# Expert keys beside the scatter: both parts of x in one 512-column matmul, the two column blocks added one step later

## What is computed

```python
def peer_ffn(n, w_q, sub_keys, expert_u, expert_v):
    """PEER: 8 product-key retrieval heads over N = 128^2 single-neuron experts."""
    ...
    experts = (i1 * PEER_KEYS + i2).reshape(T, PEER_HEADS * PEER_TOPK)
    gates = jax.nn.softmax(best, axis=-1).reshape(T, PEER_HEADS * PEER_TOPK).astype(n.dtype)
    ...
        u = expert_u[eb].astype(xb.dtype)
        act = jax.nn.gelu(jnp.einsum('td,tkd->tk', xb, u), approximate=False) * gb
        return jnp.einsum('tk,tkd->td', act, expert_v[eb].astype(xb.dtype))
```

## Time and profile before

| | us |
|---|---|
| median of 3 runs | 1690.45 |
| lowest, highest | 1690.38, 1691.01 |
| the profiled execution | 1690.79 |
| its span in the profile | 1689.0 |
| PE busy | 1658.7 |
| DVE busy | 1284.7 |
| ACT busy | 1028.3 |

### The profile page before, as it was taken

One profiled execution on the slowest core, in us unless ns is written; L12 is line 12 of the kernel. 1 busy time (PEld: TensorE's weight loads), 2 busy tenths in 40 slices (PEclk: granted clock), 3 DMA queues, 4 the chain that ended last, 5 costly groups with the idle time before them and its releaser, 6 DMA issues.

```text
span 1689.0 us, 34320 instructions
## 1 busy us (share of the span) xinstructions
PE 1658.7 (98%) x10835; PEld 1499.1 (89%) x10835; DVE 1284.7 (76%) x2365; ACT 1028.3 (61%) x1626; POOL 116.5 (7%) x105
## 2 busy tenths in 40 slices
PE   8999999999999999999999999999999999999998
PEld 7998889999999999988888888899788888878886
DVE  7867763899877777777777777799777777977776
ACT  7757555667556666655545455765576667766665
POOL 0025200444000000000000000100000000000000
PEclk9999999999999999999999999999999999999999
DMA  6543464777755555477787777542455554346553
GB/s 211 174 150 101 144 218 146 229 220 227 241 195 171 173 177 176 154 248 243 240 274 241 245 238 241 178 148 88 150 171 191 189 191 148 101 158 193 191 192 113
DMA packets 113294, 315.64 MB, mean 187 GB/s; under 512 B 12640, under 2 KB 44640, under 8 KB 112848
## 3 DMA queue, kind: packets, MB, share of 16 engines
q1 hardware_dynamic: 112032, 310.43, 56.5%
q0 software_dynamic: 880, 4.06, 0.7%
q10 hardware_dynamic: 320, 0.34, 0.1%
HBM read 296.43 MB, written 18.35 MB: 186 GB/s over the span
## 4 chain that ended last, share of the span: by engine, by line
PE 94%; DVE 2%; ACT 2%; DMA 1%; issue 1%; POOL 0%; SPq 0%; ACTq 0%; DVEq 0%; POOLq 0%
PE bank L273 12%; PE bank L274 12%; PE bank L275 12%; PE bank L338 11%; PE bank L339 10%; PE bank L340 10%; PE bank L294 10%; PE bank L298 5%; PE bank L1546 3%; PE bank L2003 2%; PE bank L330 1%; PE bank L332 1%; PE bank L331 1%; DVE wlo L245 1%; DMA h<-act_spill 0%
## 5 line engine op out<-in xcount | busy, mean ns | idle before, releaser
L245 DVE TENSOR_TENSOR wlo<-raw,whi 128x1024 fp32r<-128x1024 f32 x499 | 612.8, 1231 | 133.1 <-ACT whi L237 124.8
L237 ACT ACTIVATE whi<-raw 128x1024 fp32r<-128x1024 f32 x524 | 550.4, 1053 | 19.7 <-PE bank L332 14.0
L273 PE MATMUL bank<-x,whi 128*128 128x256 f32 (+3 forms) x1728 | 504.4, 292 | 2.5 <-DVE x L486 0.7
L275 PE MATMUL bank<-x,wlo 128*128 128x256 f32 (+3 forms) x1728 | 489.4, 283 | 0.0
L274 PE MATMUL bank<-x,whi 128*128 128x256 f32 (+3 forms) x1728 | 489.3, 283 | 0.0
L273 PEld LDWEIGHTS bank<-x,whi 128*128 128x128 f32 x1728 | 330.1, 191 | 6.1 <-issue 3.1
L274 PEld LDWEIGHTS bank<-x,whi 128*128 128x128 f32 x1728 | 330.7, 191 | 0.3
L275 PEld LDWEIGHTS bank<-x,wlo 128*128 128x128 f32 x1728 | 329.9, 191 | 0.0
L338 PE MATMUL bank<-whi,yhi 128*128 128x512 f32 x816 | 319.3, 391 | 1.0 <-DVE ylo L2343 0.7
L339 PE MATMUL bank<-wlo,yhi 128*128 128x512 f32 x816 | 318.1, 390 | 0.0
L340 PE MATMUL bank<-whi,ylo 128*128 128x512 f32 x816 | 317.6, 389 | 0.0
(11 more groups left out here) (324 smaller groups left out, 1712.5 us busy)
## 6 DMA issues: line engine op xcount, KB each, us to landing
raw<-in_stream SPq DMA_DIRECT2D x524, 512.0 KB, 3.4
act_spill<-h SPq DMA_DIRECT2D x124, 128.0 KB, 3.3
h<-act_spill SPq DMA_DIRECT2D x124, 128.0 KB, 3.2
h<-in_x SPq DMA_DIRECT2D x2, 512.0 KB, 5.1
arena<-in_keys POOLq DMA_DIRECT2D x1, 1024.0 KB, 6.3
h_spill<-h SPq DMA_DIRECT2D x1, 1024.0 KB, 7.9
arena<-h_spill POOLq DMA_DIRECT2D x1, 1024.0 KB, 7.3
arena<-in_g_final POOLq DMA_DIRECT2D x1, 512.0 KB, 9.3
```

Of the source, the lines that this page charges most:

```text
L237: nc.scalar.activation(whi[:, q * 1024:(q + 1) * 1024], raw[:, q * 1024:(q + 1) * 1024], ACT.Copy).then_inc(hi_ready, 1)
L245: nc.vector.tensor_tensor(wlo[:, q * 1024:(q + 1) * 1024], raw[:, q * 1024:(q + 1) * 1024], whi[:, q * 1024:(q + 1) * 1024].bitcast(F32), ...
L273: nc.tensor.matmul(bank[b][:, 0:T], whi[:, w], xhi[:, x], start=k == 0, stop=False)
L275: last = nc.tensor.matmul(bank[b][:, 0:T], wlo[:, w], xhi[:, x], start=False, stop=k == KT - 1)
```

## The change

Slabs 63 to 126 go through `up_halves` and no longer through `up`. The first pair of one-hot matmuls then stands between the 512-column and the 256-column matmuls, and the second behind the latter. The reading of a bank, one ACT instruction before, becomes three: ACT copies the right half to `HR` (`half_out`), DVE adds the left half to it and frees the bank (`half_sum`, in the step after), and ACT applies GELU in place (`half_gelu`, one step later than before). SP writes the activation to memory when the GELU is done (`u_act`), and the first product with the gates waits for it too. What that does to the order on the engines:

ACT in the steps of the scatter, before: one reading of the bank between two splits. `whi` is a high split, `arena` the store of G.

The diff, without the loops of the last steps on DVE and SP that only follow from it:

```diff
@@ in up_halves
             else:
                 for k in range(KT):
                     long(k)
+                if between:
+                    between()
                 pe.wait_ge(lo_ready, n + 1)
                 for k in range(KT):
                     last = short(k, k == KT - 1)
@@ in pe_peer
             def step(i, r):
-                up(pe, N_U + E1, U_U + E1, i, r, 4, SEQ, between=lambda: pair(i, r, 0))
+                up_halves(pe, N_U + E1, U_U + E1, i, r, 4, between=lambda: pair(i, r, 0))
                 pair(i, r, 1)
@@ in act_peer
+            def half_out(k0, i, r):
+                q = (k0 + r) % 4
+                act.wait_ge(slabs_done, at(N_U + k0, i, r, 4) + 1 + RING)
+                act.wait_ge(spill_sem(q), rounds(k0, i, r, 4) * 16 + 16)
+                nc.scalar.activation(HR[:, q * SEQ:(q + 1) * SEQ], bank[(U_U + k0 + r) % 2][:, SEQ:2 * SEQ], ACT.Copy)\
+                    .then_inc(s("u_half"), 1)
+
+            def half_gelu(k0, i, r):
+                q = slice((k0 + r) % 4 * SEQ, ((k0 + r) % 4 + 1) * SEQ)
+                act.wait_ge(up_evac, at(U_U + k0, i, r, 4) + 1 + 2)
+                nc.scalar.activation(HR[:, q], HR[:, q], ACT.Gelu).then_inc(s("u_act"), 1)
+
             split_hi(act, N_U + E1 + AHEAD, 0, 0, 4)
-            gelu(N_U + E1, U_U + E1, 0, 0)
+            half_out(E1, 0, 0)
 
             def step2(i, r):
                 split_hi(act, N_U + E1 + 1 + AHEAD, i, r, 4)
                 g_out(i, r)
-                gelu(N_U + E1 + 1, U_U + E1 + 1, i, r)
+                half_out(E1 + 1, i, r)
+                half_gelu(E1, i, r)
 
             steps(act, SCAT - 1, 4, step2)
             g_out(0, SCAT - 1)
+            half_gelu(E1 + SCAT - 1, 0, 0)
@@ in dve_peer
+            def half_sum(k0, i, r):
+                q = slice((k0 + r) % 4 * SEQ, ((k0 + r) % 4 + 1) * SEQ)
+                dve.wait_ge(s("u_half"), at(k0 - E1, i, r, 4) + 1)
+                nc.vector.tensor_tensor(HR[:, q], HR[:, q], bank[(U_U + k0 + r) % 2][:, 0:SEQ], ALU.add)\
+                    .then_inc(up_evac, 1)
+
+            def step(k0, i, r):
+                one_token(k0, i, r, 0)
+                one_token(k0, i, r, 1)
+                split_lo(dve, N_U + E1 + k0 + AHEAD, i, r, 4)
+                if k0:
+                    half_sum(E1 + k0 - 1, i, r)
+                one_token(k0, i, r, 2)
+                one_token(k0, i, r, 3)
+                four_tokens(k0 + 1, i, r)
@@ in prod
-                    dve.wait_ge(up_evac, U_U + KEYS - KEPT + k + 1 + 2)
+                    dve.wait_ge(s("u_act"), SCAT - KEPT + 1 + k + 1) if k < KEPT - 1 else \
+                        dve.wait_ge(up_evac, U_U + KEYS + 2)
@@ in sp_peer_loads
+            def store(k0, i, r):
+                load(sp, N_U + lead + k0, i, r, 4)
+                if k0 < E1:
+                    sp.wait_ge(up_evac, at(U_U + k0, i, r, 4) + 1 + 2)
+                else:
+                    sp.wait_ge(s("u_act"), at(k0 - E1, i, r, 4) + 1)
+                q = (k0 + r) % 4
+                sp.dma_start(act_dram(i, r, k0), HR[:, q * SEQ:(q + 1) * SEQ]).then_inc(spill_sem(q), 16)
```

More of the change, by code:

```diff
@@ L281, in up, with up_halves @@
             last.then_inc(slabs_done, 1)
-        def up_halves(pe, n0, u0, i, r, U, uU=None, x_ready=None):
+        def up_halves(pe, n0, u0, i, r, U, uU=None, x_ready=None, between=None):
             n, u = at(n0, i, r, U), at(u0, i, r, U if uU is None else uU)
@@ L1774, in dve_peer, with one_token @@
                     columns()
-            def one_token(i, r, y):
-                n = i * (4 * TPS) + r * TPS + y
+            def one_token(k0, i, r, y):
+                n = i * (4 * TPS) + (k0 + r) * TPS + y
                 dve.wait_ge(s("hot_free"), n - 2 + 1 + TPS)
@@ L1788, in four_tokens @@
                                         ALU.is_equal).then_inc(s("hot_b"), 1)
[L1790 to L1796, removed]
+            def half_sum(k0, i, r):
[12 more added lines that the diff above has]
+                four_tokens(k0 + 1, i, r)
             four_tokens(0, 0, 0)
-            steps(dve, SCAT - 1, 4, step)
+            step(0, 0, 0)
+            steps(dve, SCAT - 2, 4, lambda i, r: step(1, i, r))
             last = SCAT - 1
             for y in range(TPS):
-                one_token(last // 4, last % 4, y)
+                one_token(last, 0, 0, y)
                 if y == 1:
                     split_lo(dve, N_U + KEYS - 2 + AHEAD, 0, 0, 4)
+                    half_sum(E1 + last - 1, 0, 0)
+            half_sum(E1 + last, 0, 0)
             def prod(k0, i, r):
@@ L1881, in act_dram @@
                     t["act_spill"][bass.ds(k, 1)].rearrange("a p c -> (a p) c")
[L1883 to L1893, removed]
+            def store(k0, i, r):
[6 more added lines that the diff above has]
+                sp.dma_start(act_dram(i, r, k0), HR[:, q * SEQ:(q + 1) * SEQ]).then_inc(spill_sem(q), 16)
+            steps(sp, E1 - 3, 4, lambda i, r: store(0, i, r))
+            for k in (E1 - 3, E1 - 2, E1 - 1, E1):
+                store(k, 0, 0)
+            steps(sp, KEYS - 2 * KEPT - E1 - 1, 4, lambda i, r: store(E1 + 1, i, r))
+            for k in range(KEYS - 2 * KEPT, KEYS - KEPT):
+                store(k, 0, 0)
             for k in range(KEYS - KEPT, KEYS):
```

## The result

| | before | after |
|---|---|---|
| median, us | 1690.73 | 1698.68 |
| lowest, highest | 1690.38, 1691.09 | 1698.29, 1699.03 |
| runs | 4 | 4 |
| the profiled execution | 1690.79 | 1698.81 |
| its span | 1689.0 | 1697.0 |

The ratio is 1.0047, with a 95% interval of 1.0035 to 1.0059: slower by 8.0 us, where +1.2 was forecast and the range went up to 1698.0. The clock is at its full level in both (PEclk 1.00 in the stage), so the time is not lost in the clock.

What follows compares the result with a forecast made beforehand. PE's own work was taken to bound the stage, with late one-hots then setting a 3.78 us step; -0.2 (first slabs) + 1.2 (62 steps) + 0.2 (end) = +1.2 us, forecasting 1691.7 us, range 1686.5 to 1698.0.

Steps and rivals of the forecast that it cites:

- What bounds the stage: In the 64 scatter steps, PE's own work sets the pace, 3.76 us a step; PE waits for nobody.
- the chain, link by link: From a slab's end T through ACT and DVE queues to PE's load of the last one-hot: T + 3.86.
- The 0.2 us put behind them: After the steps, the last gate store stands behind ACT's added pass and delays the first down slab: about 0.2 us.
- The two edits given one line each: In the scatter steps, the later activation write-out and SP's next slab load behind it: cost nothing.
- From the late load the first matmul of slab s+2 is 0.20 away: On PE, second one-hot pass 0.17 behind the first, slab's matmul 0.03 later; slab s+2 starts at T + 4.06.
- ACT's branch: At the head of ACT's unrolled loop, a bank read 0.10 late once in four steps: 0.025 us a step.
- The list of signs: What the trace of the steps would show if right (step 3.76 to 3.80, DVE releasing one-hots) or wrong.
- chain of two steps, halved: Slab s to s+2: 4.06 to the start plus 3.45 of PE work, 7.51 us in two steps, 3.755 each.
- the gain that could be had: PE's own step falls from 3.76 to 3.66 us through longer matmuls: 6.4 us over 64 steps.
- the upper ends: Slower wake-up, restarted matmul row, add without overlap, loop's 0.13 before the high split: step 3.92, +9.9 us all together.
- The second rival: In the pair behind each slab, a late PE restarts dearly: step 3.85, 1696.0 us; chance 0.27 with other upper ends.
- the second pair of every step released by DVE: The one-hot pair behind each slab waits for DVE, half a microsecond of slack becoming a lack of about 0.25.

Runs made afterwards that it cites:

- the kernel with both moves: Changed kernel with ACT's GELU moved behind the high split and gate store, and DVE's add behind one-hots 2 and 3; 1686.96 us.
- the shape alone: Kernel before with the new 512-column matmul shape, without the copy and add; GELU reads the right half of the bank; 1686.41 us.

## Why the prediction was wrong

**What held.** What bounds the stage; that the added passes hide as work and still stand in the queues ahead of the one-hots; the chain, link by link, T + 3.78 for 3.81 to the one-hots' end, T + 4.08 for 4.06 to the next slab with the branch away; that all is settled in the steps. The 0.2 us put behind them don't show: from the start of slab 127 to the first matmul with `expert_v` it is 2.95 us before (711.23 to 714.18) and 2.94 after (718.80 to 721.74). The two edits given one line each (the write-out, SP's later load) cost nothing that a trace shows: without either loop the stage is explained by the chain alone.

**The step that failed** is in "What it adds and where it waits": "From the late load the first matmul of slab s+2 is 0.20 away". It is 0.25 wherever no branch follows, the one-hots late or not. Once in four steps PE's own loop branch stands between them, and it is 0.56, and the sum has no term for it. I read ACT's branch out of the rows and charged it with 0.025 a step, which measured 0.025 (15.22 less 2 x 7.56, by four). PE's branch left no mark in the rows of before, because the last one-hot ended 0.79 us ahead of the slab's first load and the branch needs 0.6, and I took what left no mark for free. The rule that the prediction itself uses, to say what hides a cost and what it is when the cover goes, was applied to the moved instructions and not to those that stay. It was worth 0.32 in four steps, 0.08 a step. The list of signs had room for it ("idle pieces over 0.3 a step, restart or an unseen wait"), the sum had not.

The Trainium skill (Perfetto Trace Analysis, Tensor Engine Instruction) draws a matmul or weight load that waits as sitting in a wait queue, with the sequencer free to decode the next instruction. In this trace no control instruction ran past a waiting load: the ALU_OP of line 114 is at 578.524, the load that waited at 578.523. By the page's picture the branch would have been through before; the measurement decides. Nor is it the loads themselves that are not passed: in the kernel with both moves the ALU_OP at 573.199 ran ahead of all loads of the last two one-hots (573.240 on), 0.05 us after the last one-hot was done.

**The sizes.** The 8.0 us are, in 63 steps:

| term | forecast, a step | measured, a step | difference in all |
|---|---|---|---|
| chain of two steps, halved | 3.755 | 3.780 | +1.6 |
| ACT's branch | 0.025 | 0.025 | 0 |
| PE's branch | none | 0.080 | +5.0 |
| all | 3.78 | 3.885 | +6.6 |

With the forecast's +1.2 that makes 7.8. The 0.05 too little in the chain of two steps is mostly PE's own part from a slab's start: to T it took 3.49 (577.17 to 579.46 + 1.20 in the kernel with the loop written out), not 3.45. The full step without any wait is 3.69, not 3.66, as the shape alone shows; so the gain that could be had was 0.07 a step, an estimated 4.4 us and not 6.4, and the shape alone gave 3.8. The long matmuls are 0.231 apart in this stage and 0.227 in the feed-forward stage from whose rows I took them.

**The bounds.** They reached to 3.92 a step, and 3.887 lies inside, but for a wrong reason: the upper ends were a wake-up, a restart, an add that doesn't overlap. None came true; that the bounds were wide enough for the step is luck. The second rival, a dear restart, gives 1696.0, near the result too, and is refuted: a late start costs no more than one in time (0.25 us both). A kernel slower by more than a measurement can tell was given 0.285.

**The pattern.** The prediction has the second pair of every step released by DVE. It is every second one. The two chains, of even and of odd slabs, don't stay evenly spaced: one runs up to PE's own pace (3.69) behind the other and then waits no more, and the mean is the same.

## What to carry to other kernels

On PE, the engine's own loop branch cost nothing only while its queue ran far enough ahead of the work; before an edit makes an operand of that engine late, look up the records of its branch and registers and price them as exposed. Where the operand's slack drops below what the branch needs (here about 0.6 us, and 0.32 was lost each time at none), write the loop out or shorten the chain; moving the branch to another step of the same period gave nothing back that could be told. Judge the slack from the end of the last operand to the start of the work behind the branch, not to the operand's own use. An added pass on an idle engine should stand behind the instruction that the critical engine needs next: the same two passes one place later turned +8.0 us into -3.2.

## What the runs showed of the hardware

- A weight load whose semaphore is not there yet holds PE's sequencer: no register or branch instruction behind it ran until the last one-hot was done. In the eight kernels with a branch on PE the loop's first instruction starts 0.05 to 0.08 us after the end of the last one-hot, in every pass between 480 and 705 us. Loads that are behind only because the array is busy don't hold it (573.199 before 573.240).
- The branch of a loop on PE: 208 ns for the branch itself, and 0.60 to 0.66 us from the end of the last one-hot to the next slab's first load in seven of them (0.79 in the kernel before, where the load waits for the array); 0.32 of it in the open when the one-hots were late, 0.03 with the shape alone.
- A late start of PE costs nothing beyond the wait: from the last one-hot's load to the slab's first matmul it is 0.25 us, late or not.
- On ACT the branch costs 0.09 us in the instruction behind it, and the first read of the bank in the new iteration comes 0.09 late too.
- PE's busy time hides starving: 1.3 us of idle time where PE took some 12 us longer than its own work. Late pairs show as rows of 0.74 for 0.61.
